# A two-block network on one core: twelve convolution taps moved to GpSimd, six gate tiles in split form, one mean earlier

## The reference

```python
n = rmsnorm(h, norm_g[i])
z = n @ w_in[i] + b_in[i]
(c_val, c_glu, c_gate, p_in, p_gate, q, k, v, a_gate, qi, ki, wi) = jnp.split(z, cut, axis=-1)
ya = conv_module(c_val, c_glu, ...) * jax.nn.silu(c_gate)
yb = pool_mixer(p_in, ...) * jax.nn.silu(p_gate)
...
yc = sparse_attention(q, k, v, qi, ki, wi) * jax.nn.silu(a_gate)
h = h + jnp.concatenate([ya, yb, yc], axis=-1) @ w_out[i]
h = h + (p[i] @ ple_w[i]) * jax.nn.sigmoid(h @ ple_gate_w[i])

def conv_module(val, glu, dw_w, dw_b, ln_g, ln_b, pw_w, pw_b):
    u = val * jax.nn.sigmoid(glu)
    u = lax.conv_general_dilated(u, dw_w[:, None, :], ...) + dw_b   # 31 taps, each channel by itself
    u = jax.nn.silu(layernorm(u, ln_g, ln_b))
    return u @ pw_w + pw_b
```

## Time and profile before

| | |
|---|---|
| median of 3 runs | 1458.97 us (1457.33 to 1460.35) |
| the profiled execution's own time | 1460.37 us |
| its span | 1458.5 us |
| TensorE busy | 1389.7 us, 95% of the span |
| VectorE busy | 1043.5 us, 72% |
| ScalarE busy | 709.1 us, 49% |
| GpSimd busy | 48.0 us, 3% |
| mean granted TensorE clock | 0.978 |

### The profile page before, as it was taken

The page is one execution under the profiler, slowest core; times in us unless marked ns, Lnnn a source line. Parts: engine busy times, 40 slices in busy tenths (PEclk is TensorE's granted clock), DMA queues, the critical chain, the costliest instruction groups (busy, mean ns, idle before and its releaser), DMA issues.

```text
span 1458.5 us, 21897 instructions
## 1 busy us (share of the span) xinstructions
PE 1389.7 (95%) x8497; PEld 1196.5 (82%) x8497; DVE 1043.5 (72%) x1993; ACT 709.1 (49%) x1191; POOL 48.0 (3%) x67
## 2 busy tenths in 40 slices
PE   6999999998999999898999999999899988899997
PEld 5787887878978886677888888888788867899997
DVE  6697686977679885646798898666443756788854
ACT  5537566366544642634543444322245636566643
POOL 0000000000000012000000000000000210000000
PEclk9999999999999999898999999999899999999999
DMA  7643456325376521031445445577333331355552
GB/s 261 217 152 123 157 180 218 130 89 174 129 253 221 173 97 49 15 106 39 145 159 164 155 159 169 189 252 252 104 114 105 114 102 62 127 193 181 181 187 95
DMA packets 61943, 218.52 MB, mean 150 GB/s; under 512 B 7024, under 2 KB 9072, under 8 KB 61456
## 3 DMA queue, kind: packets, MB, share of 16 engines
q1 hardware_dynamic: 59200, 205.55, 42.1%
q0 software_dynamic: 2496, 11.56, 2.3%
q10 hardware_dynamic: 144, 0.00, 0.0%
HBM read 216.04 MB, written 1.05 MB: 149 GB/s over the span
## 4 chain that ended last, share of the span: by engine, by line
PE 83%; ACT 7%; DVE 6%; issue 2%; DMA 2%; DVEq 0%; ACTq 0%; SPq 0%
PE bank L574 19%; PE bank L576 19%; PE bank L575 19%; PE bank L590 5%; ACT WHI L1326 2%; PE bank L1150 1%; PE bank L635 1%; DVE WLO L1863 1%; DMA RAWB<-in_ws 1%; PE bank L637 1%; PE bank L636 1%; DVE DP L1956 1%; ACT L1326 1%; PE bank L612 1%; PE bank L613 1%
## 5 line engine op out<-in xcount | busy, mean ns | idle before, releaser
L1863 DVE TENSOR_TENSOR WLO<-RAWB,WHI 128x1024 fp32r<-128x1024 f32 (+1 forms) x276 | 328.7, 1193 | 202.3 <-ACT WHI L1326 201.5
L574 PE MATMUL bank<-NHI,WHI 128*128 128x256 f32 (+1 forms) x1392 | 464.0, 333 | 8.7 <-DVE WLO L1863 7.6
L575 PE MATMUL bank<-NLO,WHI 128*128 128x256 f32 (+1 forms) x1392 | 458.0, 329 | 0.0
L576 PE MATMUL bank<-NHI,WLO 128*128 128x256 f32 (+1 forms) x1392 | 458.0, 329 | 0.0
L1326 ACT ACTIVATE WHI<-RAWB 128x1024 fp32r<-128x1024 f32 (+1 forms) x276 | 283.2, 1029 | 203.8 <-PE bank L576 119.6
L574 PEld LDWEIGHTS bank<-NHI,WHI 128*128 128x128 f32 x1392 | 265.0, 190 | 42.5 <-issue 11.1
L575 PEld LDWEIGHTS bank<-NLO,WHI 128*128 128x128 f32 x1392 | 265.2, 190 | 24.7 <-issue 1.4
L576 PEld LDWEIGHTS bank<-NHI,WLO 128*128 128x128 f32 x1392 | 265.0, 190 | 23.7
L1956 DVE CUSTOM_DVE_ANT_0 DP<-RAWB,CREP,PRM 128x1024 f32<-128x1024 f32 x120 | 153.9, 1283 | 6.4 <-DMA RAWB<-in_ws 0.3
L1326 ACT ACTIVATE CF<-bank,PRM 128x512 f32<-128x512 f32 (+1 forms) x88 | 59.1, 671 | 177.7 <-PE bank L576 174.6
L574 PE MATMUL bank<-HHI,WHI 128*128 128x512 f32 (+1 forms) x352 | 119.1, 338 | 0.0
(11 more groups left out here) (326 smaller groups left out, 1920.6 us busy)
## 6 DMA issues: line engine op xcount, KB each, us to landing
RAWB<-in_ws SPq DMA_DIRECT2D x364, 512.0 KB, 3.4
RAWB<-in_ws SPq DMA_DIRECT2D x32, 384.0 KB, 3.6
NB<-in_nab POOLq DMA_DIRECT2D x12, 256.0 KB, 3.4
CREP<-in_crep POOLq DMA_DIRECT2D x2, 1024.0 KB, 6.5
K<-in_c POOLq DMA_DIRECT2D x2, 896.0 KB, 5.7
K<-in_c POOLq DMA_DIRECT2D x1, 1344.0 KB, 9.1
X<-in_xt SPq DMA_DIRECT2D x4, 256.0 KB, 4.8
X<-in_xt POOLq DMA_DIRECT2D x1, 1024.0 KB, 7.7
```

Of the source, the lines that this page charges most:

```text
L574: nc.tensor.matmul(o, hi[:, w], xh, start=(i == 0), stop=False)
L575: nc.tensor.matmul(o, hi[:, w], xl, start=False, stop=False)
L576: ins = nc.tensor.matmul(o, lo[:, w], xh, start=False, stop=(i == slabs - 1))
L1863: V.tensor_tensor(WLO[:, k % SPL, 0:w], RAWB[:, u % RAW, 0:w], WHI[:, k % SPL, 0:w].bitcast(F32), ALU.subtract).then_inc(S("lo_ready"), 1)
```

## The change

GpSimd now computes taps 19 to 30 into a sum of its own, CP, with CQ as scratch. It starts when DVE has written UP (a new semaphore, `up_made`). A tap is two multiplications of 128x256, one for each slab, and, from the second tap on, one addition of 128x512. DVE keeps taps 0 to 18, spread anew over the items, and adds CP to its own sum behind item 8 (`add_pool_taps`, a wait for `pool_taps` and one addition of 128x512). Tiles 19 to 24 (the second half of the attention gate, the convolution gate and the pooling gate) take the split form. The first `channel_mean` moves ahead of `attend` at t = 23.

```diff
-NATIVE_FROM = Z1["kb"]
+NATIVE_TILES = range(Z1["kb"], Z1["agate"] + 2)
...
+POOL_TAPS = range(19, CONV_K)
 TAPS_AT = {10: (0, 1)}
-TAPS_BESIDE = {0: (1, 2), 2: (3, 4), 3: (7, 8), 4: (11, 12), 5: (15, 16), 6: (19, 20), 7: (23, 24), 8: (27, 28)}
-TAPS_AFTER = {1: (2, 3), 2: (4, 7), 3: (8, 11), 4: (12, 15), 5: (16, 19), 6: (20, 23), 7: (24, 27), 8: (28, CONV_K)}
+TAPS_BESIDE = {0: (1, 2), 2: (3, 4), 3: (6, 7), 4: (9, 10), 5: (12, 13), 6: (14, 15), 7: (17, 18)}
+TAPS_AFTER = {1: (2, 3), 2: (4, 6), 3: (7, 9), 4: (10, 12), 5: (13, 14), 6: (15, 17), 7: (18, 19)}
...
                 nc.gpsimd.tensor_tensor(PB[:], prm_col(f"poolb{l}", 0, 2), prm_col(f"pools{l}", 0, 2), ALU.mult).then_inc(S("pb_ready"), 1)
+                pool.wait_ge(S("up_made"), l + 1)
+                for k in POOL_TAPS:
+                    for m in range(2):
+                        w, src = prm_col(f"dww{l}", m * CONV_K + k), UP[:, m, k:k + T]
+                        if k == POOL_TAPS[0]:
+                            ins = nc.gpsimd.tensor_scalar(CP[:, m, :], src, w, None, ALU.mult)
+                        else:
+                            ins = nc.gpsimd.tensor_scalar(CQ[:, m, :], src, w, None, ALU.mult)
+                    if k > POOL_TAPS[0]:
+                        ins.then_inc(S("pool_chain"), 1)
+                        pool.wait_ge(S("pool_chain"), me.nth("pool_chain"))
+                        ins = nc.gpsimd.tensor_tensor(CP[:], CP[:], CQ[:], ALU.add)
+                    if k < POOL_TAPS[-1]:
+                        ins.then_inc(S("pool_chain"), 1)
+                        pool.wait_ge(S("pool_chain"), me.nth("pool_chain"))
+                    else:
+                        ins.then_inc(S("pool_taps"), 1)
                 pool.wait_ge(S("z_freed"), NZ1 * l + 18)
...
-                    elif t < NATIVE_FROM:
+                    elif t in NATIVE_TILES:
+                        native(b, "z_freed")
+                    else:
                         fm(KS, T, x_new, "z_freed", "x_split" if t == UNDIVIDED else None, b=b)
-                    else:
-                        native(b, "z_freed")
...
+                    if t == 23:
+                        channel_mean(4, CV, "conv_ready", "xc_ready")
                     if t >= ATTEND_FROM:
                         attend(t - ATTEND_FROM)
...
-                    if t == 23:
-                        channel_mean(4, CV, "conv_ready", "xc_ready")
...
+                def add_pool_taps():
+
+                    dve.wait_ge(S("pool_taps"), l + 1)
+                    V.tensor_tensor(CV[:], CV[:], CP[:], ALU.add).then_inc(S("conv_ready"), 1)
+                    dve.wait_ge(S("conv_ready"), me.nth("conv_ready"))
...
                     if k in TAPS_AFTER:
                         taps(*TAPS_AFTER[k])
+                    if k == n:
+                        add_pool_taps()
```

More of the change, by code:

```diff
@@ L140, in stream @@
         for t in range(NZ1):
-            add([UNIT], t >= NATIVE_FROM)
+            add([UNIT], t in NATIVE_TILES)
             rows(2 if t in ROWS1 else 0)
@@ L246, in build @@
         CT = sb(st, "CT", [P, 2, T])
+        CP = sb(st, "CP", [P, 2, T])
+        CQ = sb(st, "CQ", [P, 2, T])
         PD = sb(st, "PD", [P, 2, T])
@@ L2086, in taps @@
                                 ins = V.scalar_tensor_tensor(CV[:, m, :], src, w, CV[:, m, :], ALU.mult, ALU.add)
-                        if k < CONV_K - 1:
-                            ins.then_inc(S("dve_chain"), 1)
-                            dve.wait_ge(S("dve_chain"), me.nth("dve_chain"))
-                        else:
-                            ins.then_inc(S("conv_ready"), 1)
-                            dve.wait_ge(S("conv_ready"), me.nth("conv_ready"))
+                        ins.then_inc(S("dve_chain"), 1)
+                        dve.wait_ge(S("dve_chain"), me.nth("dve_chain"))
+                def add_pool_taps():
+                    dve.wait_ge(S("pool_taps"), l + 1)
+                    V.tensor_tensor(CV[:], CV[:], CP[:], ALU.add).then_inc(S("conv_ready"), 1)
+                    dve.wait_ge(S("conv_ready"), me.nth("conv_ready"))
                 def gated(src, slabs, g0, first):
@@ L2153, in _ @@
                         dve.wait_ge(S("z_freed"), zb + Z1["val"] + 2)
-                        V.tensor_tensor(UP[:, :, CONV_K - 1:], Z[:, Z1["val"]:Z1["val"] + 2, :], SG[:], ALU.mult).then_inc(S("dve_chain"), 1)
-                        dve.wait_ge(S("dve_chain"), me.nth("dve_chain"))
+                        V.tensor_tensor(UP[:, :, CONV_K - 1:], Z[:, Z1["val"]:Z1["val"] + 2, :], SG[:], ALU.mult).then_inc(S("up_made"), 1)
+                        dve.wait_ge(S("up_made"), l + 1)
                     if t == 2:
```

## The result

The changed kernel takes 1471.68 us (median of 4 runs, 1470.15 to 1472.43) against 1459.66 for the kernel before on the same chip (4 runs, 1457.33 to 1462.9). The ratio is 1.0078, with a 95% interval of 1.0067 to 1.009. It is slower by some 12 us; the forecast was 1460.6, in a range from 1453.5 to 1468.0. The prediction was wrong.

What follows compares the result with a forecast made beforehand. TensorE was taken to bound 79.7 to 130.3 us, then ACT to 144.8. The terms -5.4 + 4.0 + 3.0 gave +1.6 us on the profiled 1460.37, so 1460.6 for the median, range 1453.5 to 1468.0.

Steps and rivals of the forecast that it cites:

- the price of a meeting: DVE instruction with two SBUF inputs meeting a GpSimd SBUF read: 0.3 us longer, from a row measured beside copies.
- the cost of WHI and WLO: Six extra split-tile units on ACT and DVE, t = 17 to 22: costed at nothing, as covered by free time.
- GpSimd's part of the sum: TensorE's loss from DVE being late at item 1: 4.0 us in layer 0 and 3.0 in layer 1.
- rival 2: DVE at 63 to 87 and 250 to 274 us: long additions block, 0.5 us a meeting, sum +8.0, 1467.0 us; chance 0.24.
- My formula: The whole sum over two layers as 32w - 8.0 us, with w the price of a meeting; zero at w = 0.25.
- its sum of +11.2: Sum by the skill's shared-read-interface rule: addition 1.1 us, multiplication 0.4, mean meeting 0.6; given under rival 2.
- the gain of 5.4: TensorE's saving from split tiles 19 to 22, ahead of the turn to ACT: 0.67 us each, 5.4 in two layers.
- Rival 3: WHIs and WLOs of t = 19 to 22 tie attention loop to ACT: 0.5 us an item, 4 us more, 1464.6; chance 0.06.
- Even twice this is hidden: GpSimd's twelve taps, put at 30 us from 61.3, would finish before DVE asks for the sum at about 128.
- The taps that left DVE: 24 fewer DVE instructions, balance 3.3 us less DVE work a layer: nothing for TensorE, since DVE already waited for it.
- the mean's move: The mean goes ahead of one value product, 0.58 us on TensorE: nothing gained, nothing lost.
- Waits at items 6 and 7: Sign of error: the forecast is wrong if TensorE waits at items 5 to 7.

Runs made afterwards that it cites:

- e1: The changed kernel with tiles 19 to 24 back in native form, GpSimd still doing twelve taps: 1475.75 us, 1.010 of the kernel before.
- e3: The changed kernel with GpSimd's taps 19 to 30 left out and tiles 19 to 24 native: 1460.55 us, 1.0 of the kernel before.
- e5: The changed kernel with GpSimd's taps left out and, from item 3 on, WLO moved behind the maximum: 1456.36 us, 0.9967 of the kernel before.
- e12: As e11, but only tiles 19 and 20 split and fewer taps at the end: 1458.83 us, 0.999 of the kernel before.
- e11: The changed kernel with all 31 taps on DVE, none on GpSimd, and WLO behind the maximum: 1471.04 us, 1.0066 of the kernel before.

## Why the prediction was wrong

Two terms of its sum failed, the price of a meeting by 4.1 us and the cost of WHI and WLO by 6.7; by S the sum should have been +12.3 and was put at +1.6.

1. **"For the price of a meeting I take 0.3 us, the row."** This is the mis-sized term: GpSimd's part of the sum was 7.0 us in two layers and measured 11.1 (e1 less e3). The row was right for what it showed, a copy with one input in SBUF; the multiplications, which also have one, cost DVE no more than 0.24 us. It said nothing of the additions, and they hold DVE for what is left of their 1.27 us. So the mechanism was that of rival 2, "the additions stand in the way for their whole length", which had a chance of 0.24; what the prediction set against it, that "the reading part, not the whole, seems to block", did not hold for an addition. My formula gives the 11.1 us at 32w - 2.6, so at w = 0.43 over all counted instructions: near rival 2's 0.5. That mean hides the pattern: seven meetings of 0.8 to 1.1 us in layer 0 and six of 0.5 to 1.1 in layer 1, and the rest nearly unhurt. The count was wrong as well: "a DVE instruction with two SBUF inputs" left out TENSOR_SCALAR with one (1.72 for 0.74), and the work went on to 104 us, not 96, past item 1. In layer 1 one of the meetings holds a small GR of DVE (1.18 us for 0.17) ahead of all that was counted, and TensorE waits 2.0 us for GR, 1.0 before. The rule in the Trainium skill's "SBUF — State Buffer" was the better guide for the additions, but not for the multiplications. That its sum of +11.2 came so near is luck: its mean of 0.6 a meeting makes GpSimd's part 16.6 us by the same formula, and the gain of 5.4 that did not come covers that.

2. **"I cost both at nothing"**, of the six WHI and WLO. The working looked at each engine's free time (ScalarE had 8.8 us), and not at the order in which one hands to the other. The WLO stood ahead of the maximum in DVE's order, the WHI behind the probabilities in ScalarE's, and this closed the ring, 17.7 us for three items where TensorE needed 17.0 even with native tiles. The gain of 5.4 us became 0.2 without GpSimd's work and a loss of 1.3 beside it. Rival 3 named this with 0.5 us an item and a chance of 0.06; it was 0.65 us a tile without GpSimd's work and 0.84 beside it, so all that a tile could gain.

3. **GpSimd's prices.** A multiplication was put at 0.40 us and took 0.91, a tap 2.4 and took 3.1 (1.82 + 1.27). "Even twice this is hidden" held: DVE's addition of CP found the sum ready. The addition was the dear one for DVE all the same.

4. **What held.** A split tile saves TensorE time wherever nothing swallows it, 0.59 us a tile instead of the 0.67 read from the earlier trace rows (3.06 us beside the items, not 2.98; e5 4.7 us of 5.4, e12 2.4 of 2.7). The taps that left DVE gave TensorE nothing (e3, S 0.0). ScalarE is again the limit behind tile 22 (13.66 of 14.10 us), and the mean's move cost nothing there; only with DVE late behind the last item it did (e11). GpSimd's load of X, late behind the taps, was waited for by nobody. TensorE's waits about items 0 and 1 were foreseen at 3 to 4 us, at the turning and for ScalarE; in layer 0 they came to 5.5, of which 2.1 are at the turning of items 0 to 2, and the rest are waits for DVE, at the scores and at L846. Waits at items 6 and 7, named as a sign of error, came.

## What to carry over

Work moved to GpSimd is not free while DVE is full: in this kernel each DVE instruction with SBUF inputs that started in a GpSimd addition of two SBUF arrays paid for the rest of that addition, and one that started in a multiplication by a value per partition almost nothing. So count the two-input instructions first, and put the work where DVE's own steps have that much room, if it is to be moved at all. When an engine is made faster inside a loop that passes between several, add up the ring by the order of each queue, not by busy shares: if it turns as slowly as the engine did, nothing is gained until one instruction leaves the ring.

## What had not been expected of the hardware

- A GpSimd multiplication of 256 elements by a value per partition takes 0.91 us, while an addition of 512 elements takes 1.27: by element the one-input form is dearer (3.6 ns against 2.5).
- What holds DVE is GpSimd's addition, not its multiplication: at 73.32 to 75.06 a WLO and two more started in multiplications and took 1.23, 0.68 and 0.68 us, and the one at 75.84, in an addition, took 1.58. In multiplications it is GpSimd that loses (3.34 for 1.82 us).
- Waits of TensorE up to 1.4 us left the granted clock at 1.00; two of 2.26 and 2.39 us, 3 us apart, were followed by 0.56 to 0.59 for some 8 us, and one of 5.05 us by 6 us at 0.50.
